# Odd layer of a four-layer block: the second half's exponential first, its reciprocal beside the other, a head's small constant ahead of its squares

## The reference, cut to what matters

```
for each head h and each block i of 128 queries:
    s1, s2 = q1 @ k1.T / 8, q2 @ k2.T / 8          # masked: 64-token chunks, keys up to the query's chunk
    p1, p2 = softmax(s1), softmax(s2)
    a  = p1 - lam * p2
    o  = a @ v
o = rms_norm(o, subln_g) * (1 - lambda_init)
y = (o * silu(gate)) @ w_out ;  return x + y
```

## Time and profile before

| | |
|---|---|
| time, median of 3 runs | 2024.1 us (2024.04 to 2028.17) |
| the profiled execution: its time | 2023.36 us |
| the profiled execution: its span | 2021.5 us |
| granted TensorE clock, mean over the span | 0.991 of full speed |
| share of the span: PE, DVE, ACT, POOL | 96%, 53%, 49%, 39% |
| share of the chain that ended last: PE, DVE, ACT | 79%, 14%, 4% |

### The profile page before, as it was taken

One profiled execution on the slowest core, in us unless ns is written; L12 is line 12 of the kernel. 1 busy time (PEld: TensorE's weight loads), 2 busy tenths in 40 slices (PEclk: granted clock), 3 DMA queues, 4 the chain that ended last, 5 costly groups with the idle time before them and its releaser, 6 DMA issues.

```text
span 2021.5 us, 25706 instructions
## 1 busy us (share of the span) xinstructions
PE 1942.8 (96%) x10008; PEld 1615.0 (80%) x10008; DVE 1076.5 (53%) x1934; ACT 989.9 (49%) x1737; POOL 792.4 (39%) x367
## 2 busy tenths in 40 slices
PE   6999999989999999999999999999999999999997
PEld 5778888867778877777788888888878888888886
DVE  4366553378754677766737464412546584344214
ACT  5465635367743555556526444422555464444323
POOL 3431234454433333333253444444352334444442
PEclk9999999999999999999999999999999999999999
DMA  5321123222222222222132322333221223222332
GB/s 185 96 66 43 54 82 94 89 84 58 84 63 87 72 73 77 71 71 80 57 104 79 105 94 95 101 88 102 64 80 53 77 69 105 98 94 96 95 94 71
DMA packets 55193, 169.30 MB, mean 84 GB/s; under 512 B 7072, under 2 KB 13856, under 8 KB 54944
## 3 DMA queue, kind: packets, MB, share of 16 engines
q1 hardware_dynamic: 54784, 166.92, 26.3%
q10 hardware_dynamic: 288, 0.74, 0.1%
HBM read 158.72 MB, written 2.10 MB: 80 GB/s over the span
## 4 chain that ended last, share of the span: by engine, by line
PE 79%; DVE 14%; ACT 4%; issue 2%; DMA 1%; POOL 0%; SPq 0%; DVEq 0%; ACTq 0%
PE ps L1839 19%; PE ps L1842 19%; PE ps L1840 19%; PE ps L1899 2%; PE ps L1884 2%; PE ps L1851 2%; PE ps L1852 2%; PE ps L1854 2%; DVE tmp L2392 1%; PE ps L1892 1%; PE ps L1867 1%; PE ps L1866 1%; PE ps L1864 1%; DVE s_xbc L2371 1%; PE ps L1873 1%
## 5 line engine op out<-in xcount | busy, mean ns | idle before, releaser
L2567 POOL TENSOR_TENSOR wl<-st,wh 128x1024 fp32r<-128x1024 f32 (+2 forms) x311 | 722.2, 2324 | 1155.1 <-ACT wh L2005 1154.8
L2005 ACT ACTIVATE wh<-st 128x1024 fp32r<-128x1024 f32 (+2 forms) x311 | 314.1, 1011 | 517.3 <-PE ps L1842 454.3
L1839 PE MATMUL ps<-xh,wh 128*128 128x512 f32 x1368 | 555.8, 406 | 2.1 <-DVE tmp L2259 2.1
L1842 PE MATMUL ps<-xh,wl 128*128 128x512 f32 x1368 | 534.5, 391 | 0.0
L1840 PE MATMUL ps<-xl,wh 128*128 128x512 f32 x1368 | 533.5, 390 | 0.0
L1839 PEld LDWEIGHTS ps<-xh,wh 128*128 128x128 f32 x1368 | 257.3, 188 | 60.0 <-issue 8.3
L1842 PEld LDWEIGHTS ps<-xh,wl 128*128 128x128 f32 x1368 | 256.8, 188 | 56.0 <-POOL wl L2567 0.9
L1840 PEld LDWEIGHTS ps<-xl,wh 128*128 128x128 f32 x1368 | 257.6, 188 | 49.4 <-issue 2.6
L2526 DVE SCALAR_TENSOR_TENSOR tmp<-ps,vec,tmp 128x510 f32<-128x510 f32 (+1 forms) x176 | 131.3, 749 | 223.4 <-ACT tmp L2184 220.5
L2484 DVE SCALAR_TENSOR_TENSOR res<-res,ps 128x512 f32<-128x512 f32 (+1 forms) x37 | 22.7, 615 | 207.5 <-PE ps L1842 199.8
L1839 PE MATMUL ps<-fa_h,wh 128*128 128x512 f32 x308 | 120.7, 392 | 0.0
(11 more groups left out here) (276 smaller groups left out, 3555.8 us busy)
## 6 DMA issues: line engine op xcount, KB each, us to landing
st<-in_f_up SPq DMA_DIRECT2D x88, 512.0 KB, 3.3
st<-in_s_xbc SPq DMA_DIRECT2D x32, 512.0 KB, 3.5
st<-in_f_dn SPq DMA_DIRECT2D x32, 512.0 KB, 3.5
st<-in_o_fm SPq DMA_DIRECT2D x24, 512.0 KB, 3.5
st<-in_e_fm SPq DMA_DIRECT2D x21, 512.0 KB, 3.5
st<-in_s_z SPq DMA_DIRECT2D x16, 512.0 KB, 3.5
st<-in_s_out SPq DMA_DIRECT2D x16, 512.0 KB, 3.4
tmp<-tmp SPq DMA_DIRECT2D x100, 64.0 KB, 2.0
```

The source lines that it names most:

```text
L1839: e.matmul(u.bank.ap, hi, x.h[:, kk, :], start=first, stop=False)
L1842: e.matmul(u.bank.ap, lo, x.h[:, kk, :], start=False, stop=last).then_inc(S["mm"], 1)
L2005: e.activation(P.mem["wh"][w.m % NWR][:, 0:w.n], P.mem["stage"][w.m % NSTAGE][:, 0:w.n], ACT.Copy).then_inc(S["w_hi"], 1)
L2567: e.tensor_tensor(P.mem["wl"][w.m % NWR][:, 0:w.n], P.mem["stage"][w.m % NSTAGE][:, 0:w.n], P.mem["wh"][w.m % NWR][:, 0:w.n].bitcast(F32), ...
```

## The change

In `attend` the loop over the two halves runs backwards, so ScalarE does the second half's exponential first. The reciprocal waits only for that one, and is written to the second column of the pair of minima, which only that exponential reads. The factor `mix_c` now waits for both exponentials and the reciprocal. In `finish`, `sub_e` is yielded ahead of the four squares and waits for the PV steps of the head and for its buffer; `sub_a` waits for it and for the squares. The number of instructions of each kind is the same.

```diff
--- before.py
+++ after.py
@@ -1168,13 +1168,13 @@
     def finish(h, ob, mn, sm, rr, to):
         ends = []
         j = yield from P.taken(P.tmp)
+        s1 = sm.ap.rearrange("p (i a) -> p i a", a=2)[:, :, 0]
+        e = yield ("sub_e", rr.ap[:, 4:8], s1, 128 * 1e-6, [to, rr.freed])
         for i in range(4):
             ends.append((yield ("sub_sq", cols(j.ap, i), ob.ap[:, i * 128:(i + 1) * 128], rr.ap[:, i:i + 1], to,
                                 rr.freed, j.freed)))
         j.release(*ends)
-        s1 = sm.ap.rearrange("p (i a) -> p i a", a=2)[:, :, 0]
-        t = yield ("sub_e", rr.ap[:, 4:8], s1, 128 * 1e-6, ends)
-        t = yield ("sub_a", rr.ap[:, 4:8], rr.ap[:, 0:4], t)
+        t = yield ("sub_a", rr.ap[:, 4:8], rr.ap[:, 0:4], [e] + ends)
         sm.release(t)
         mn.release(t)
         t, a = yield from P.rstd_g(rr.ap[:, 4:8], rr.ap[:, 4:8], 1.0 / 128, 0.0, t, [])
@@ -1229,15 +1229,16 @@
                 t = yield ("mn", mn.ap[:, 2 * i:2 * i + 2], g.s, t, mn.freed, 2 * n)
                 yield from g.probs(pr)
                 ex = []
-                for a in range(2):
+                for a in (1, 0):
                     j = 2 * i + a
                     ex.append((yield ("exp", g.p[a], g.s[:, a, :], mn.ap[:, j:j + 1], sm.ap[:, j:j + 1], t,
                                       [g.freed(g.p_uses), sm.freed], n)))
                 for u in g.uses:
                     u.release(*ex)
-                r = yield ("rec2", mn.ap[:, 2 * i:2 * i + 1], sm.ap[:, 2 * i + 1:2 * i + 2], ex)
-                c = yield ("mix_c", mn.ap[:, 2 * i:2 * i + 1], sm.ap[:, 2 * i:2 * i + 1], lam, [r, tlam])
-                d = yield ("mix_d", g.p[0], g.p[1], mn.ap[:, 2 * i:2 * i + 1], [c] + ex, n)
+                f = mn.ap[:, 2 * i + 1:2 * i + 2]
+                r = yield ("rec2", f, sm.ap[:, 2 * i + 1:2 * i + 2], ex[0:1])
+                c = yield ("mix_c", f, sm.ap[:, 2 * i:2 * i + 1], lam, [r, tlam] + ex)
+                d = yield ("mix_d", g.p[0], g.p[1], f, [c] + ex, n)
                 if not g.small:
                     g.p_uses[1].release(d)
                 P.start(1, back(h, i, g, d, ob, mn, sm, rr, to))
```

## The result

The changed kernel is slower: 2034.76 us median of 5 runs (2032.43 to 2037.55), against 2025.52 for 5 runs of the kernel before in the same series (2024.04 to 2028.17). The ratio is 1.0045, 95% interval 1.0034 to 1.0057. The profiled execution took 2032.43 us, 9.1 us more than the profiled one of before.

What follows compares the result with a forecast made beforehand. TensorE was taken as the bound, busy 96% of the span, with only idle time to win. The terms -1.6 - 0.2 - 1.1 + 1.0 gave -1.9 us, from 2024.1 to 2022.2 us; range 2017.5 to 2028.0 us.

Steps and rivals of the forecast that it cites:

- Everything else in the new lists I cost at nothing net: Odd attention's new order: trios only change places, no net cost; moved GpSimd holds get 2 us either way.
- `sub_e` ahead of the squares: In `finish`: nobody waits in heads 0 to 6; head 7's output turn comes earlier, 0.2 us won.
- The reciprocal leaves the chain: Before the flips: `mix_c` starts 0.20 us earlier, 8 of 28 waits shortened in full, 1.6 us won.
- Head 7, block 2: Its PV step waited 1.08 us for the copy; a turn and a trio now stand between, 1.1 us won.
- Head 6, block 0: Three trios and a turn leave the place between scores and flip; TensorE stands there, 1.0 us lost.
- The tail: After the last turn 2.23 us idle stays, as does the 20 us stretch with mean clock 0.83, costing 3.4 us.
- What would show it: Signs in the changed profile: flips' waits on the mix from 17.0 to about 15 us, attention idle time about 15.5 us.
- signs of being wrong: Holds several microseconds off 9.6 us, waits at 128-key blocks' flips in most heads, or a 1.2 GHz stretch coming or going.
- held anyway: Rival, 22%: GpSimd holds the mixes TensorE waits for longest, so only the lists' terms, -0.3, are left: 2023.8 us.
- Too little cover: Rival, 14%: the eight 128-key blocks lost 16 trios, each needs 1.0 us more: +5.1, 2029.2 us.

Runs made afterwards that it cites:

- Freed of both: Changed kernel, same lists, `mix_c` reading one tensor and `sub_e` written as a reciprocal of the four sums (epsilon and square left out): 2024.3 us, 0.9998 of before.
- The `finish` part alone: Kernel before with only `finish` changed (`sub_e` yielded ahead of the squares), `attend` as before: 2032.34 us, ratio 1.0038.
- In the old lists: Kernel before's engine lists, but for the swap of the two exponentials in each pair, with the changed kernel's waits: 2024.02 us, ratio 1.000.
- without the low parts: GpSimd's low part of weights 50 to 73 done for 32 of 1024 columns: kernel before 2015.57 us (0.9949), changed kernel 2014.12 us (0.9945).
- the redrawn kernel before: Kernel before, same work and waits, planner's estimate of the reciprocal 132 for 152 ns, so its lists are drawn anew: 2037.57 us, ratio 1.0058.

## Why the prediction was wrong

- **"Everything else in the new lists I cost at nothing net"**, with 2 us either way for the holds: this is the step that failed, through its bound. That the holds move was said; that they could come to 9 us was not. The range of 2 us was one mix held once more or less. But the lists moved 6.2 us of holds onto `mix_c` and 6.6 us onto `sub_e`, and took 3.0 us from the 256-wide mix; with the other widths (+1.8 us at 384 columns, -1.0 at 512) the sum is 10.6 us more. Freed of both, the same lists take 0.9998 of before.
- **"*`sub_e` ahead of the squares*", nobody waits in heads 0 to 6**: wrong too. I had looked at whether the PV step ends in time, and priced `sub_e` at its free 0.2 us. I had written down the rule for `mix_c` and `mix_d` and didn't apply it to `sub_e`, which has two tensors as well. In its old place it stood behind the squares, mostly clear of GpSimd (median 158 ns); in the new one its median is 1337 ns and the next block's reciprocal stands behind it. Freeing it is worth 1.0015 to 0.9998, some 3 us, with `mix_c` free, and 1.0045 to 1.0038 without; the last pair's intervals overlap. The `finish` part alone shows the same early `sub_e` nearly free (2.9 us), so its earlier place alone doesn't hold it; what GpSimd does beside it in the combined lists does.
- **The reciprocal leaves the chain, -1.6 us**: the mechanism is there (0.10 us from accumulator read to `mix_c`). In the old lists it took the flip's array waits from 6.2 us to 4.4 in the profile, and the time to 1.000 (0.999 to 1.001): compatible with -1.6 us, not shown by it. In the new lists, with its wait taken back, 1.006 in place of 1.0045 points the same way, within the overlap of the intervals.
- **Head 7, block 2, -1.1 us**: right, the PV step at 583.46 has no idle time before it. **Head 6, block 0, +1.0 us**: right without the hold (2.45 - 1.43 = 1.02). With `mix_c` and `sub_e` free the mix itself is held at this place, and the flip still waits 2.19 us.
- **The tail**: the idle time after the last turn is 2.23 us, as said. `sub_e` left it. The 20 us with a mean clock of 0.83 have a clock of 1.00 now. A shorter stretch at the lower clock comes later, 600 to 620 has 0.91, and two more have come in the attention: 480 to 500 and 540 to 560 have 0.91 each (see the last section). Over the three windows that is 3 x 0.09 x 20 = 5.4 us of TensorE's time against 0.17 x 20 = 3.4 before.
- **What would show it**: the flips wait 26.7 us for the mix, where about 15 was said, and TensorE's idle time in the attention is 216 - 190.04 = 26.0 us, where 15.5 was said. Both moved the other way. Two of the signs of being wrong came together: holds that differ by several microseconds, and waits at the flips of the 128-key blocks in seven of the eight heads. These seven make up 8.2 of the array's 12.2 us before the flip, against 1.5 us before.
- **The rivals**: *held anyway* named the right engine, but took the holds as fixed in number. *Too little cover* ended on the right side for a reason that two runs refute: without the low parts, and with `mix_c` and `sub_e` free, the same cover is enough. Its place was right, though: a hold costs TensorE most at the 128-key blocks, which have 12 trios for cover in place of 28. With both steps free the array's idle time there is 3.3 us in place of 8.2, of which 2.19 in head 6. Its case of 2029.2 us and the range's upper end of 2028.0 both lay below the result. One of its sums is off: less the microsecond already counted, six blocks give -1.9 + 5.0 = +3.1, and seven are needed for +4.1.

What stays open: the `finish` part alone. In its profile `mix_c` takes 13.9 us and the array's idle time before the flips is 5.1 us, hardly unlike before, but one place stands out:

```profile
482.41 5.11 POOL L2567 TENSOR_TENSOR wl<-st,wh 128x1024 fp32r<-128x1024 f32 x2 [8.25 <-ACT wh L2005]
...
483.53 1.79 DVE L2227 TENSOR_TENSOR yl<-tmp,yh 128x512 fp32r<-128x512 f32 x1
...
485.35 2.72 DVE L2539 TENSOR_TENSOR kz<-tmp,kz 64x512 fp32r<-64x512 f32 x1
...
488.10 0.75 DVE L2259 SCALAR_TENSOR_TENSOR tmp<-ps,vec,tmp 128x512 f32<-128x512 f32 x1
...
488.90 0.79 PE L1839 MATMUL ps<-xh,wh 128*128 128x512 f32 x1 [4.39 <-DVE tmp L2259]
```

Two low parts in a row hold a head's low part and a key's, 1.1 and 2.0 us over the 0.68 that free ones take, and a trio waits 4.39 us for the bank. Its mean clock in the attention is 0.95 against 0.98, which over 216 us is 6.5 us of TensorE's time. Holds of other instructions and the clock behind them may be part of it; no run took these away. The clock is not all of it: of the five runs of this kernel the one with a mean clock of 0.991 took 2030.22 us, while the runs of the kernel before with 0.991 on the same chip took 2024.77 to 2025.46. Nor was it tried to run the redrawn kernel before with neither `mix_c`'s holds nor the low parts, so what its lists cost on their own has no mechanism yet.

## What to carry to other kernels

Where a planner or scheduler decides the order, price a change by the order that comes out and not by the instructions that it shortens: 20 ns in an estimate cost as much as the worst edit here. For each instruction that moves, ask what the neighbouring engine does at its new place, and count every instruction of the exposed form, the small ones above all: a 0.16 us step that waits 2 us for another engine delays all that is queued behind it. An exposed small instruction can be put in a form that isn't held, if one computes the same; but look where the hold goes then. In the kernel before it went to the mix behind, and nothing was won.

## What the runs showed of the hardware

- In the places shown a hold of a small instruction ends with GpSimd's, not after a share of it (469.43 and 469.42; 468.04 and 468.01), and costs up to 2 us on an instruction of 0.16 us. Which forms are held is more than "two tensors": a TENSOR_SCALAR of 128x4 is (up to 2.08 us, mean 1.16), a TENSOR_SCALAR of 128x1 (at most 0.277 us in 32) and RECIPROCALs of 128x1 and 128x4 (at most 0.179 us in 8) are not. The Trainium skill (GPSIMD Engine Reference, section Key points) names VectorE instructions in a 2-port perf mode beside those with two SBUF inputs. The Trainium skill (VectorE: DVE Perf Modes, section What auto-detection actually checks) gives the two-port mode where a single source and the destination are in SBUF and their outermost non-unit dimensions are both even or equal. The held TENSOR_SCALAR of four elements agrees with this, and one of one element has no such dimension. The RECIPROCAL of four elements has the same shape and isn't held (0.18 us inside GpSimd's instruction at 468.20), so the shape alone doesn't decide.
- The clock. In the `finish` kernel the 4.39 us wait is followed by trios at half speed; the window reads

```profile
480.00:500.00 20.00, 14.96 (x69) 11.65 (x68) 16.45 (x28) 11.56 (x34) 10.18 (x6) 0.83 0.28 80
```

  where the kernel before has 1.00 in the same window, and in the changed kernel idle times of 2.50 us (before 481.05) and 2.45 us (before 550.93) lie ahead of the slow matmuls of the windows with 0.91. In such a window TensorE runs part of the time at 1.2 in place of 2.4 GHz: behind the 4.39 us wait the matmuls of 512 columns start 0.43 us apart (489.92 to 490.35), later 0.23 (493.63 to 493.86). That a hold is so paid twice is likely but not shown: with `mix_c` and `sub_e` free, 440 to 460 and 540 to 560 have 0.91 too, the latter behind the 2.19 us wait. I had looked for this only in the tail.
